# Hi and lo weight products of the feed-forward gate and up units: two runs of eight, or alternating block by block

## The reference

```python
def _swiglu(h, w_gate, w_up, w_down):          # h: 256 x 1024, w_gate, w_up: 1024 x 2816
    return (jax.nn.silu(h @ w_gate) * (h @ w_up)) @ w_down

def second_block(x, ...):
    for l in range(DEPTH):                     # DEPTH = 2; the first block has the same three parts
        y = _swiglu(_modulate(x, sh1, sc1), ffn1_w_gate[l], ffn1_w_up[l], ffn1_w_down[l])
        x = _post_norm(x, y, g1, FFN_RES, ln_gain[l, 0], ln_bias[l, 0])
        ...
        y = _swiglu(_modulate(x, sh3, sc3), ffn2_w_gate[l], ffn2_w_up[l], ffn2_w_down[l])
```

## Time and profile before

| | |
|---|---|
| median of three runs | 2171.44 us |
| profiled execution, first to last instruction | 2169.3 us |
| TensorE matmuls, busy | 2125.2 us, 12850 instructions |
| TensorE weight loads, busy | 1864.8 us |
| VectorE, ScalarE busy | 1653.5 us, 1182.4 us |
| chain that ended last | 88% TensorE, 7% VectorE, 3% ScalarE |

### The profile page before, as it was taken

One profiled execution on the slowest core, in us unless ns is written; L12 is line 12 of the kernel. 1 busy time (PEld: TensorE's weight loads), 2 busy tenths in 40 slices (PEclk: granted clock), 3 DMA queues, 4 the chain that ended last, 5 costly groups with the idle time before them and its releaser, 6 DMA issues.

```text
span 2169.3 us, 34586 instructions
## 1 busy us (share of the span) xinstructions
PE 2125.2 (98%) x12850; PEld 1864.8 (86%) x12850; DVE 1653.5 (76%) x2161; ACT 1182.4 (55%) x1589; POOL 73.5 (3%) x70
## 2 busy tenths in 40 slices
PE   8999999999999999999999999999999999999997
PEld 7888999888888889988888888988888888898886
DVE  6877897787778788977877877867787557876657
ACT  5545545654655574465556546546546445656544
POOL 0000200000000003000000000100000000000000
PEclk9999999999999999999999999999999999999999
DMA  8775322577487642238765775437764555443553
GB/s 313 292 281 204 128 79 98 214 282 279 169 325 267 260 156 98 79 112 315 267 255 215 285 280 205 137 105 281 277 252 171 194 200 213 156 136 137 183 194 145
DMA packets 59413, 446.65 MB, mean 206 GB/s; under 512 B 6977, under 2 KB 7361, under 8 KB 8897
## 3 DMA queue, kind: packets, MB, share of 16 engines
q1 hardware_dynamic: 59328, 445.50, 55.2%
HBM read 444.42 MB, written 1.05 MB: 205 GB/s over the span
## 4 chain that ended last, share of the span: by engine, by line
PE 88%; DVE 7%; ACT 3%; DMA 1%; issue 1%; POOL 0%; SPq 0%; DVEq 0%; ACTq 0%
PE ps L249 28%; PE ps L358 15%; PE ps L254 15%; PE ps L364 8%; PE ps L265 3%; PE ps L307 2%; PE ps L313 2%; PE ps L308 2%; PE ps L339 2%; PE ps L230 1%; PE ps L236 1%; PE ps L231 1%; DVE w_lo L206 1%; DMA raw<-in_g 1%; DVE tok L777 1%; PE ps L1196 1%
## 5 line engine op out<-in xcount | busy, mean ns | idle before, releaser
L206 DVE TENSOR_TENSOR w_lo<-raw,w_hi 128x1024 fp32r<-128x1024 f32 x670 | 813.4, 1235 | 274.6 <-ACT w_hi L199 273.8
L199 ACT ACTIVATE w_hi<-raw 128x1024 fp32r<-128x1024 f32 x670 | 693.7, 1052 | 411.2 <-PE ps L364 133.7
L249 PE MATMUL ps<-hT,w_hi 128*128 128x512 f32 x2688 | 671.3, 392 | 0.5 <-ACT w_hi L199 0.5
L249 PEld LDWEIGHTS ps<-hT,w_hi 128*128 128x128 f32 x2688 | 487.9, 189 | 91.4 <-ACT w_hi L199 1.1
L254 PEld LDWEIGHTS ps<-hT,w_lo 128*128 128x128 f32 x2688 | 366.7, 190 | 26.2
L254 PE MATMUL ps<-hT,w_lo 128*128 128x256 f32 x2688 | 374.8, 282 | 0.0
L358 PE MATMUL ps<-w_hi,act_hi 128*128 128x512 f32 x672 | 208.9, 392 | 0.0
L358 PE MATMUL ps<-w_hi,act_lo 128*128 128x512 f32 x672 | 207.6, 390 | 0.0
L364 PE MATMUL ps<-w_lo,act_hi 128*128 128x512 f32 x672 | 179.6, 389 | 0.0
L2081 DVE SCALAR_TENSOR_TENSOR arena<-arena,cond 128x1024 f32<-128x1024 f32 x144 | 168.5, 1221 | 2.7 <-DMA arena<-in_w_ada 2.7
L358 PEld LDWEIGHTS ps<-w_hi,act_lo 128*128 128x128 f32 x672 | 126.2, 188 | 27.5
(11 more groups left out here) (370 smaller groups left out, 2447.5 us busy)
## 6 DMA issues: line engine op xcount, KB each, us to landing
raw<-in_u SPq DMA_DIRECT2D x88, 1024.0 KB, 4.9
raw<-in_d SPq DMA_DIRECT2D x88, 1024.0 KB, 6.9
raw<-in_g SPq DMA_DIRECT2D x87, 1024.0 KB, 4.8
arena<-in_w_ada SPq DMA_DIRECT2D x48, 1536.0 KB, 7.5
raw<-in_w_in SPq DMA_DIRECT2D x54, 1024.0 KB, 4.9
raw<-in_w_out SPq DMA_DIRECT2D x16, 1024.0 KB, 4.9
rows<-in_rows SPq DMA_DIRECT2D x12, 1024.0 KB, 9.0
arena<-in_con SPq DMA_DIRECT2D x1, 1344.0 KB, 10.8
```

What stands on the lines that cost most here:

```text
L199: nc.scalar.activation(w_hi[:, buf, 0:width], raw[:, slot, half * UNIT:half * UNIT + width], ACT.Copy).then_inc(unit_hi, 1)
L206: nc.vector.tensor_tensor(w_lo[:, buf, 0:width], raw[:, slot, half * UNIT:half * UNIT + width], w_hi[:, buf, 0:width].bitcast(F32), ALU.su ...
L249: nc.tensor.matmul(o, h_[:, k, c], hT[:, :, 4 * half + k, :], start=(half == k == 0), stop=False)
```

## The change

In `wide_unit` each lo product comes right behind the hi product that uses the same block position, and TensorE waits once, ahead of the unit's first product, for `unit_lo`. Since VectorE adds to `unit_lo` only after it has read the hi part, that wait covers both parts. The number of matmuls, their shapes, their operands and the banks they add into are as before, and so are all other functions.

```diff
         h_, l_ = (w[:, buf, :].rearrange("p (k n) -> p k n", k=4) for w in (w_hi, w_lo))
-        unit_ready(pe, unit_hi, B, j)
+        unit_ready(pe, unit_lo, B, j)
         for s in range(2):
             o, c = ps[:, bank + s, :].rearrange("p (z t) -> p z t", z=2), slice(s * P, (s + 1) * P)
             for k in range(4):
                 nc.tensor.matmul(o, h_[:, k, c], hT[:, :, 4 * half + k, :], start=(half == k == 0), stop=False)
-        unit_ready(pe, unit_lo, B, j)
-        for s in range(2):
-            c = slice(s * P, (s + 1) * P)
-            for k in range(4):
                 last = nc.tensor.matmul(ps[:, bank + s, 0:SEQ], l_[:, k, c], hT_hi[:, 4 * half + k, :], start=False,
                                         stop=(half == 1 and k == 3))
         last.then_inc(unit_done, 1)
```

## The result

The changed kernel takes 2186.02 us (median of 5 runs, 2185.78 to 2187.68) against 2171.44 us before: 0.7% slower, ratio 1.0070 with a 95% interval of 1.0059 to 1.0081. The forecast was 2168.4 us, 3 us faster; the kernel moved the other way. The time lies inside the stated range, near its end, on the side that the prediction gave to its third rival.

The account below looks back on a forecast made before the run. TensorE's start-to-start matmul distance was taken to bound the kernel. Order and changes of width, about -5 us, plus late lo waits, +2, gave -3 us: 2171.4 to 2168.4 us, range 2150 to 2187.

Parts of the forecast that it names:

- What bounds the kernel: In `wide_unit`: TensorE's distance from one matmul's start to the next; L249 and L254 hold 28% and 15% of the span.
- Settled paces: In `wide_unit`: 0.2265 us per hi and 0.120 per lo matmul to the next start, whoever comes next; 2.772 us a unit.
- The changes of width: Hi/lo switches in `wide_unit`, two a unit before, sixteen after: pair 0.346 us, 2.77 a unit, about -5 us in all.
- The down units: Down units, unchanged code: 12 matmuls stay at 2.72 to 2.75 us; at the low end up to 2 us less.
- Rival 3: TensorE in `wide_unit` never leaves the slow state: hi stays at 0.235, lo at 0.120; 2176 to 2193 us, chance 0.23.
- Rival 2: TensorE in `wide_unit` never falls into the slow state: hi stays at 0.2265, every lo takes 0.113; 2150 us, chance 0.26.
- Rival 4: In `wide_unit`, order changes nothing but the waits: +2 us, 2173.5 us, chance 0.11.
- the Trainium skill's rule: Isolated matmul gap N / 2.4 + 2.5 ns, 216 and 109 ns; a pair is 325 ns in either order.
- The wait: Unit start waiting for the lo part: 1.25 us late at 43.23, 0.93 at 1165.71, settled rounds free; +2.2 us.
- Rival 5: Waits for the lo part in settled rounds too, at up's first unit: +8 us, 2176 us, chance 0.04.

## Why the prediction was wrong, point by point

- **What bounds the kernel**: right. TensorE's distance from start to start was the thing to read, and the loss is there.
- **Settled paces** (0.2265 and 0.120, 0.3465 a pair): right as settled paces; with one width throughout they hold in any order of the weight parts.
- **The changes of width**: this is the step that failed, in the sentence "If each matmul's distance depends on the one just before it, an alternating pair is 0.233 + 0.113 = 0.346 us". The pair is 0.3533. The distance depends on more than the matmul just before: a hi product behind a lo one is at 233 ns after a run of eight lo products and at 233, 236 or 241 when they alternate. Each of my two distances was read just behind a long run, with the array settled; alternating, hi products average 0.2367 and lo products 0.1167. The 0.236 was in the trace, as the second hi product behind a lo run, and I gave it to the rival only. The 241 was nowhere in it. Over the 336 units the term was -5 us and came out at +12.
- **The down units** were put at nothing in my value, and their 12 matmuls were to stay within 2.75 us. The order ahead of them reaches into them: 2.78 us for the first one of a round, +2.6 us in the launch.
- **Rival 3**, the array that never settles, is what happened. Its pair at the end of its range was 0.355; the hi products came out above its 0.235 and the lo products stayed a little short, as the argument against it said, so the pair was 0.3533 and the time 2186 in its span of 2176 to 2193. The chance of 0.23 was too low against 0.36 for a value that rested on carrying two single distances over to a pattern that the trace did not contain.
- **Rival 2** fell, with the reason given for it: alternating does not spare the hi stream, and more cover for the load is worth nothing (0.2267 at 512 columns in both orders; 0.4064 and not 0.400 with 384).
- **Rival 4 and the Trainium skill's rule.** By the Trainium skill's rule for the isolated gap ("TensorE: Matmul & The Clock Gate", section "Back-to-back issue gap"), which has no term for what ran before, order is free. The runs disagree: same work, 2167 to 2187 us by order alone. Its form, a fixed addition to N / 2.4, fits the settled distances, with 13 ns in place of its 2.5.
- **The wait**: 2.2 us were forecast, 1.3 us came. The first place was right (start at 44.53 us in the timeline, 44.48 forecast), and so were the free settled rounds. But TensorE came to it 0.8 us later than before, for the most part because of the slow start of this execution, so the wait cost 0.5 us there and not 1.25. The second place was wrong. It was not at 1166 but at 1999.86 us (0.9 us, where 0.93 were forecast for 1166), and there the lo part had been 0.1 us early in the kernel before. Which unit comes late hangs on when its weights land. Here ScalarE waited 1.34 us for them, in the kernel before 0.42; at the place near 1166 it was 0.58 and 1.41.
- **Rival 5**: did not happen; there are no waits in settled rounds.

## What to carry to other kernels

A distance read at a single change (of width, here) is not the distance in a stream made of changes. Where the trace doesn't contain a pattern, give as much weight to the slowest distance near a change as to the one right at it, and run the pattern before counting on a sum. Look also at what follows the changed stretch: the down units lost time though nothing in them had changed.

Runs of eight with every second unit turned round, so that runs of one width meet at the border, were the fastest order here, and one by one the slowest; between them the length of the run is no guide. A wait moved ahead by eight matmuls may be almost free. Its cost is in the few places where the operand is late, and the list of waits gives it, less what the engine idled there before.

## What the runs showed of the hardware

- fp32r products, each with its own load of 128 columns, at the 2.4 GHz level: settled distance 120 ns for 256 columns (11.51 / 96 us), 226.7 for 512 (9.07 / 40 us), 173 for 384 (the last two of eight, by their starts). All three are N / 2.4 + 13.3 ns within 1 ns, worked out from these figures.
- After a change of width the distance does not go to its settled value at once: behind a run of 256-column products it is 233, 236, 228, 232, 231 ns and then 227, in the gate and up units and, within 1 ns, in the down units. In the alternating kernel it runs in a cycle of three pairs, 1.06 us, which is 20 ns over the settled 1.04.
- The loss is not a matter of how many changes there are: 0.05 us over settled a round with 16 returns in runs of two, 0.15 with 8 in runs of four. It does not come from the PSUM bank, the source of the loads, their cover, or the waits. What inside TensorE it is, and why runs of two are so cheap, stays open.
